# Reciprocal root of the retention norm: exponential of a logarithm on ScalarE in place of a square root and four reciprocals on VectorE

## The reference

```python
def retention_out(o, g):
    o = o * lax.rsqrt(jnp.mean(o * o, -1, keepdims=True) + EPS)
    return o.reshape(o.shape[0], o.shape[1], -1).astype(g.dtype) * jax.nn.silu(g)
```

## Time and profile before

| what | value |
|---|---|
| median of 3 runs | 2582.36 us (2581.95 to 2583.49) |
| profiled execution, its own time | 2581.57 us |
| its span | 2579.9 us |
| TensorE busy | 2443.2 us, 95% of the span |
| VectorE busy | 1417.5 us, 55% |
| ScalarE busy | 877.3 us, 34% |
| GpSimd busy | 127.4 us, 5% |
| stage of the change | about 895 to 1060 us of the span |

### The profile page before, as it was taken

One profiled execution on the slowest core, in us unless ns is written; L12 is line 12 of the kernel. 1 busy time (PEld: TensorE's weight loads), 2 busy tenths in 40 slices (PEclk: granted clock), 3 DMA queues, 4 the chain that ended last, 5 costly groups with the idle time before them and its releaser, 6 DMA issues. The chain is left out here.

```text
span 2579.9 us, 31749 instructions
## 1 busy us (share of the span) xinstructions
PE 2443.2 (95%) x11762; PEld 1963.0 (76%) x11762; DVE 1417.5 (55%) x1968; ACT 877.3 (34%) x1287; POOL 127.4 (5%) x216
## 2 busy tenths in 40 slices
PE   5899999999899889999999999999999999999997
PEld 2488888899877644678888878888878677788886
DVE  4576843575563487663346763473465397532334
ACT  1422122454541366542222242222345313422222
POOL 1011200000000021000001000010000000000000
PEclk8999999999999999889999989999989999999999
DMA  7477842345421200123247523472222123223222
GB/s 287 179 260 265 311 142 73 123 151 192 145 94 66 72 1 1 49 99 98 86 147 267 171 88 103 137 273 90 73 99 98 60 86 100 65 90 104 100 74 74
DMA packets 94976, 322.11 MB, mean 125 GB/s; under 512 B 11408, under 2 KB 11824, under 8 KB 93072
## 3 DMA queue, kind: packets, MB, share of 16 engines
q1 hardware_dynamic: 67824, 221.75, 25.3%
q0 software_dynamic: 26032, 97.60, 11.2%
q10 hardware_dynamic: 1008, 1.25, 0.1%
HBM read 312.16 MB, written 8.39 MB: 124 GB/s over the span
## 5 line engine op out<-in xcount | busy, mean ns | idle before, releaser
L501 PE MATMUL psum<-h_hi,w_hi 128*128 128x512 f32 (+1 forms) x2256 | 855.6, 379 | 32.8 <-DVE h_lo L1674 13.3
L503 PE MATMUL psum<-h_hi,w_lo 128*128 128x512 f32 (+1 forms) x2256 | 846.7, 375 | 0.0
L502 PE MATMUL psum<-h_lo,w_hi 128*128 128x512 f32 (+1 forms) x2256 | 846.7, 375 | 0.0
L1456 DVE TENSOR_TENSOR w_lo<-raw,w_hi 128x1024 fp32r<-128x1024 f32 (+2 forms) x442 | 470.6, 1100 | 93.5 <-ACT w_hi L1020 90.7
L501 PEld LDWEIGHTS psum<-h_hi,w_hi 128*128 128x128 f32 x2256 | 429.5, 190 | 117.3 <-issue 27.4
L1020 ACT ACTIVATE w_hi<-raw 128x1024 fp32r<-128x1024 f32 (+2 forms) x442 | 406.0, 951 | 268.7 <-PE psum L503 223.4
L503 PEld LDWEIGHTS psum<-h_hi,w_lo 128*128 128x128 f32 x2256 | 429.0, 190 | 76.4
L502 PEld LDWEIGHTS psum<-h_lo,w_hi 128*128 128x128 f32 x2256 | 429.7, 190 | 74.9 <-issue 1.4
L501 PE MATMUL psum<-act_hi,w_hi 128*128 128x512 f32 (+1 forms) x880 | 331.3, 376 | 9.3 <-issue 5.2
L503 PE MATMUL psum<-act_hi,w_lo 128*128 128x512 f32 (+1 forms) x880 | 329.6, 375 | 0.0
L502 PE MATMUL psum<-act_lo,w_hi 128*128 128x512 f32 (+1 forms) x880 | 329.5, 374 | 0.0
(11 more groups left out here) (278 smaller groups left out, 1916.1 us busy)
## 6 DMA issues: line engine op xcount, KB each, us to landing
raw<-in_gate_up SPq DMA_DIRECT2D x220, 512.0 KB, 4.2
mod_raw<-in_w_mod POOLq DMA_DIRECT2D x168, 512.0 KB, 5.3
raw<-in_down_a SPq DMA_DIRECT2D x80, 384.0 KB, 3.7
raw<-in_down_b SPq DMA_DIRECT2D x80, 320.0 KB, 3.1
raw<-in_hy_in SPq DMA_DIRECT2D x24, 512.0 KB, 3.4
raw<-in_mix_in SPq DMA_DIRECT2D x22, 512.0 KB, 3.5
filt_dram<-made SPq DMA_DIRECT2D x6, 1024.0 KB, 3.9
taper<-in_decay SPq DMA_DIRECT2D x8, 512.0 KB, 7.6
```

What stands on the lines that cost most here:

```text
L501: pe.matmul(out, w_hi[:, slot, c:c + P], hi, start=start, stop=False)
L502: pe.matmul(out, w_hi[:, slot, c:c + P], lo, start=False, stop=False)
L503: return pe.matmul(out, w_lo[:, slot, c:c + P], hi, start=False, stop=stop)
L1456: ins = dve.tensor_tensor(w_lo[:, slot, 0:cols], raw[:, slot, 0:cols], w_hi[:, slot, 0:cols].bitcast(F32), ALU.subtract)
```

## The change

The square root becomes a natural logarithm, and a second activation, exp(-0.5 x), stands right behind it on ScalarE: together they give the reciprocal root. The four reciprocals on VectorE go. The two products (`finish`) move from step e+5 to e+2, behind `weigh`; ScalarE's high half moves to the end of step e+2 and VectorE's low half to step e+3. The loop has 35 steps in place of 36.

```diff
-INVERTED = 3
-MIX_STEPS = PAIR_END[-1] + INVERTED + 4
+MIX_STEPS = max(UNITS + 3, PAIR_END[-1] + 4)
...
                 def root(t):
                     act.wait_ge(osum_ready, t + 1)
-                    act.activation(full[:, 1, :], psum[:, 7, :], ACT.Sqrt, bias=eps[:, 0:1],
-                                   scale=1.0 / HEAD).then_inc(orms_ready, 1)
+                    act.activation(full[:, 1, :], psum[:, 7, :], ACT.Ln, bias=eps[:, 0:1],
+                                   scale=1.0 / HEAD).then_inc(orms_log, 1)
+                    act.wait_ge(orms_log, t + 1)
+                    act.activation(full[:, 0, :], full[:, 1, :], ACT.Exp, scale=-0.5).then_inc(orms_ready, 1)
...
-                    if s - INVERTED - 2 in PAIR_END:
-                        ret_out(PAIR_END.index(s - INVERTED - 2))
+                    if s - 2 in PAIR_END:
+                        ret_out(PAIR_END.index(s - 2))
...
-                def invert(t, part):
+                def finish(t):
 
                     dve.wait_ge(orms_ready, t + 1)
-                    part = slice(part * P, part * P + P)
-                    dve.reciprocal(full[:, 0, part], full[:, 1, part]).then_inc(dve_step, 1)
-                    at["step"] += 1
-
-                def finish(t):
-
-                    dve.wait_ge(dve_step, at["step"])
...
-                    if s - INVERTED - 3 in PAIR_END:
-                        ret_out(PAIR_END.index(s - INVERTED - 3))
+                    if s - 3 in PAIR_END:
+                        ret_out(PAIR_END.index(s - 3))
...
-                    for part in range(4):
-                        if s - 2 - part in PAIR_END:
-                            invert(PAIR_END.index(s - 2 - part), part)
-                    if s - 2 - INVERTED in PAIR_END:
-                        finish(PAIR_END.index(s - 2 - INVERTED))
+                    if s - 2 in PAIR_END:
+                        finish(PAIR_END.index(s - 2))
```

More of the change, by code:

```diff
@@ L387, in build @@
         back_ready, g_ready, g_hi_ready, g_split = map(sem, ("back_ready", "g_ready", "g_hi_ready", "g_split"))
+        orms_log = sem("orms_log")
         osq_ready, osum_ready, orms_ready, oval_ready = map(sem, ("osq_ready", "osum_ready", "orms_ready", "oval_ready"))
```

## The result

The changed kernel has a median of 2592.67 us in 7 runs (2591.43 to 2599.56), the kernel before 2581.95 in 7 runs taken with them. The ratio is 1.0052, with a 95% interval of 1.0042 to 1.0061, which is 11 to 16 us. The forecast was 7.5 us, 0.29%: the direction is right, the size was too small. The median lies inside the range given, but the ratio applied to the 2582.36 from which I started gives 2595.8, above its end. A second set of runs of the same changed kernel gave 1.0043 (1.003 to 1.0056). One run of the experiments, of the kernel that keeps TensorE at work, took 3536.65 us at a mean granted clock of 0.65; its ratio leaves it out.

What follows compares the result with a forecast made beforehand. TensorE, busy 95% of the span, was taken to bound the kernel, so the stage's delays pass one for one. Pairs 1 to 4 leave 2.24, 1.44, 1.44 and 2.41, sum 7.5 us, giving 2589.9; range 2585 to 2595.

Steps and rivals of the forecast that it cites:

- What bounds the stage: TensorE, busy 95% of the span, has no slack, so the changed stage's gain or loss reaches the end in full.
- The ring: In the stage, a cycle over three engines sets the pace, TensorE nearest its limit, busy 140.4 of 165 us.
- The root step: Logarithm, table load and exponential stand ahead of L1296 on ScalarE: next take 1.97 us later, four times, 7.9 us.
- more clock lost: Rival, 0.17: clock falls behind longer TensorE waits, 2.6 us each, one or two more: 2592.5 to 2595 us.
- The finishing steps: At e+2, products and ScalarE's copy delay L1296: 0.79 us in pairs 1, 3; 1.66 in pair 2; 0.44 in pair 4.
- Given back: Products gone from step e+5 let takes and transposes start earlier: 0.52, 2.19, 1.32 and 0 us in pairs 1 to 4.
- the fall of the earlier trace: Before the change, the clock was 0.51 from 997 to 1002; a rival (0.27) had this fall not come, −2.6 us.
- One table set: Rival, 0.03: in root steps one load serves logarithm and exponential, L1296 0.67 us late, sum 5.2 lower, 2584.7 us.
- VectorE is the bound: Rival, 0.05: VectorE's list sets the stage's pace, 12 removed reciprocals give 10.3 us, moved products more: about 2575 us.

Runs made afterwards that it cites:

- the copies later: The changed kernel with the retention's two copies out (ScalarE's high half, VectorE's low half) one step later: 2592.22 us, ratio 1.004.
- load and exponential: The kernel before with the changed kernel's wide exponential behind the square root, bringing the table load ahead of L1296, reciprocals kept: 2590.84 us, ratio 1.0037.

## Why the forecast was right in kind and too small

**What bounds the stage, and that it goes through one for one: right.** The ring and the wait of L848 for L1296 decided; the reciprocals were worth 2.6 to 7.2 us, not 14.9.

**The root step: right to 0.3 us in pairs 1 to 3, as a chain.** L1296 starts 2.53 behind against 2.55; the take is 1.7, 2.0 and 1.9 late with the clock held up, against 1.97. In pair 4 it is not: from take(30) to take(31) the lateness grew by 0.7 only. The kernel before ran at 0.50 from 1048.5 to 1061.5, the changed one at full clock up to the wait of that root step, so the two numbers compare clocks as well. No drain stands behind a table load here: 0.02 from its end to the next activation, in eight loads of the loop (the Trainium skill's 1.38, ScalarE: Activation LUTs, What ACT_TABLE_LOAD costs, is not in these rows).

**The clock: the step that failed.** I set it apart as a rival, "more clock lost", with a chance of 0.17, one or two falls of 2.6 us, and put it at nothing in the sum. It belongs in the sum: three falls, one in each of the root steps of pairs 1 to 3, of 1.5 to 1.6 us. That is 4.7 us, worked out as (3.3 − 1.7) + (3.6 − 2.0) + (3.4 − 1.9). A fourth, in step 13, cost another 1.65 us (below). So there were more falls than the rival had, and each was cheaper. My argument against it, that most of the waits of before passed without a fall, compared short waits with long ones: in the root steps the transposes now wait 2.37, where before they waited 0.4.

**The finishing steps: right.** +0.75 and +0.76 for pairs 1 and 3 (forecast 0.79), +1.84 for pair 2 (1.66). The copy of pair 2 was the mechanism, as the run with the copies later shows in its step 17 (5.38 us against 6.65).

**Given back: wrong in both directions, again by the clock.** In pair 1 the lateness grew by 1.1 from step 12 to 14 in place of falling by 0.5, because the clock fell behind the wait for the decay tables. TensorE there, with the change:

```profile
964.36 0.76 PE L848 MATMUL psum<-ident,probs 128*128 128x128 f32 x5 [2.71 <-ACT probs L1296]
...
968.32 1.18 PE L839 MATMUL psum<-ak,aq 128*128 128x256 f32 x2
```

The kernel before has the same wait of 2.71 and no fall behind it. Where the same wait passed without a fall after the change too, with one table set, the lateness from step 12 to 14 fell by 0.52, just what I had forecast; so the fall costs 1.65. It also came with the reciprocals merely left out of the kernel before, so the root step isn't needed for it. Of the profiles without reciprocals and with no product in this wait, seven had the fall and two did not; of the three with reciprocals, none. What ties it to VectorE's shorter list is open.

Pair 2 gave 5.5 in place of 2.2; the fall of the earlier trace rows did not come there. Pair 3 gave 2.3 in place of 1.3 by take(29), but 1.2 of it is lost again by take(30), and the kernel before with only the load moved goes down and up by the same (1.69, 0.38, 1.60) with its reciprocals in place. So that part isn't given back by the change, and where the table draws the line between pairs 3 and 4 moves 1.2 us from one to the other. The table puts both side by side, from the takes.

| pair | root step | finishing | given back | left, forecast | left, measured |
|---|---|---|---|---|---|
| 1 | 3.3 (1.97) | 0.75 (0.79) | −1.1 (0.52) | 2.24 | 5.2 |
| 2 | 3.6 (1.97) | 1.8 (1.66) | 5.5 (2.19) | 1.44 | −0.1 |
| 3 | 3.4 (1.97) | 0.8 (0.79) | 2.3 (1.32) | 1.44 | 1.8 |
| 4, with the end | | | | 2.41 | 2.1 |

The forecast is in brackets. The measured ones add up to 9.0, at the end of the loop; with 0.6 at mix_out's start and 1.1 behind they are the 10.7 of the profile. The sum of 7.5 came as near as it did by luck: the falls that I left out in the root steps and in step 13 (4.7 and 1.65 us) were in part paid for by low stretches of the kernel before that went away, those from 997 on above all.

**One table set, 0.03:** it did not come by itself, rightly; by name it does.

**A slip in a rival.** In *VectorE is the bound*, 0.8 in four finishing steps is 3.2, not 2.6; its 2575 would be some 2575.7. Nothing else hangs on it.

## What to carry to other kernels

Before an activation is added to a ring through several engines, look at what stands behind it in the same list: here the same logarithm and exponential, ahead of L1296 with the table load between them, cost 11 us more than with L1296 between the two, and 13 us more than with one table set for the stage. A stand of TensorE is priced twice where its clock falls behind it, once as the wait and once as slow products; a wait that grew from 0.4 to 2.4 us needed the second price in the sum, not in the tail. A mean clock over the stage, 0.90 and 0.92 here, doesn't tell where the falls lie. Work removed from an engine that isn't the bound should be priced by leaving it out alone (2.6 to 7.2 us of 14.9 here).

## What I had not expected of the hardware

Where TensorE waited 2.37 us in a root step of pairs 1 to 3, the clock fell to 1.2 GHz behind the wait in 10 of 12 cases (four profiles: the changed kernel twice, the copies later, load and exponential); where it waited 1.94 in the same places, in none of 3; and with products in the wait, in none of 3. In the root step of pair 4 the same four profiles waited 3.54 and the clock fell in all four; with only the load moved, a wait of 3.11 passed with no fall. Waits of 2.7 us for the decay tables in step 13 passed in some profiles with no fall (the kernel before) and were followed by one in others (the changed kernel). So the length of the wait alone doesn't decide; what else does, the runs leave open.

Two matrix products that nobody reads, in each of four root steps, made the changed kernel 7.6 us faster.
